# Two halves of the tokens around the inner norms of a two-layer encoder trunk, with half copies on ScalarE and a scaled m in PSUM

## What is computed

```python
h = rms_norm(x, norm_mix_pre[layer])
m = mixer(h, ...)                       # layer 0: RG-LRU and stick-breaking attention; layer 1: windowed GQA
x = x + rms_norm(m, norm_mix_post[layer])
h = rms_norm(x, norm_ffn_pre[layer])
u = causal_dwconv(h @ w_up, conv_w, conv_b)
f = (gelu(u[..., :2816]) * u[..., 2816:]) @ w_down
x = x + rms_norm(f, norm_ffn_post[layer])
```

## Time and profile before

| what | value |
|---|---|
| median of 3 runs | 1190.69 us (1187.4 to 1191.2) |
| the profiled execution | 1188.73 us |
| its span | 1186.9 us |
| granted TensorE clock, mean | 0.993 of full speed |
| TensorE busy | 1149.5 us |
| VectorE busy | 692.9 us |
| ScalarE busy | 486.1 us |
| GpSimd busy | 73.2 us |

### The profile page before, as it was taken

The page is one execution under the profiler, slowest core; times in us unless marked ns, Lnnn a source line. Parts: engine busy times, 40 slices in busy tenths (PEclk is TensorE's granted clock), DMA queues, the critical chain, the costliest instruction groups (busy, mean ns, idle before and its releaser), DMA issues.

```text
span 1186.9 us, 14989 instructions
## 1 busy us (share of the span) xinstructions
PE 1149.5 (97%) x5888; PEld 959.4 (81%) x5888; DVE 692.9 (58%) x840; ACT 486.1 (41%) x667; POOL 73.2 (6%) x57
## 2 busy tenths in 40 slices
PE   8999999999999999999999998899999999999997
PEld 6875777777888888888887788786888888899997
DVE  5745455558876766732228677248877766752222
ACT  4555655434533443431123229334444443433220
POOL 3000000122000000000112100033000000000000
PEclk9999999999999999999999999999999999999999
DMA  6312112222333332322321541041423333332221
GB/s 212 107 36 72 36 36 71 71 72 71 107 84 93 106 104 77 103 98 98 98 98 36 156 129 49 1 126 34 135 79 105 106 88 88 106 98 65 96 99 71
DMA packets 147477, 104.39 MB, mean 88 GB/s; under 512 B 4642, under 2 KB 144354, under 8 KB 147426
## 3 DMA queue, kind: packets, MB, share of 16 engines
q1 hardware_dynamic: 146466, 102.36, 29.0%
q10 hardware_dynamic: 960, 1.31, 0.5%
HBM read 98.02 MB, written 2.10 MB: 84 GB/s over the span
## 4 chain that ended last, share of the span: by engine, by line
PE 84%; DVE 7%; ACT 6%; issue 1%; POOL 0%; DMA 0%; POOLq 0%; SPq 0%; DVEq 0%; ACTq 0%
PE ps L1283 25%; PE ps L1285 25%; PE ps L1284 25%; DVE x L1076 3%; PE ps L1480 2%; PE ps L1468 2%; ACT hx_hi L656 1%; DVE hx_lo L1080 1%; ACT prob L772 1%; PE ps L1491 1%; PE ps L1352 1%; ACT w_hi L522 1%; PE ps L1345 1%; PE ps L1504 1%; PE ps L1660 1%
## 5 line engine op out<-in xcount | busy, mean ns | idle before, releaser
L1283 PE MATMUL ps<-hx_hi,w_hi 128*128 128x512 f32 x912 | 360.5, 395 | 2.7 <-DVE hx_lo L1080 2.5
L1284 PE MATMUL ps<-hx_lo,w_hi 128*128 128x512 f32 x912 | 355.9, 390 | 0.0
L1285 PE MATMUL ps<-hx_hi,w_lo 128*128 128x512 f32 x912 | 355.7, 390 | 0.0
L810 DVE TENSOR_TENSOR w_lo<-w_raw,w_hi 128x2048 fp32r<-128x2048 f32 (+1 forms) x90 | 201.9, 2243 | 169.5 <-ACT w_hi L522 169.4
L522 ACT ACTIVATE w_hi<-w_raw 128x2048 fp32r<-128x2048 f32 (+1 forms) x90 | 168.4, 1871 | 159.2 <-DMA w_raw<-in_ffn_w_down 113.8
L1283 PEld LDWEIGHTS ps<-hx_hi,w_hi 128*128 128x128 f32 x912 | 171.5, 188 | 45.8 <-DVE hx_lo L1080 7.2
L1285 PEld LDWEIGHTS ps<-hx_hi,w_lo 128*128 128x128 f32 x912 | 171.6, 188 | 36.3
L1284 PEld LDWEIGHTS ps<-hx_lo,w_hi 128*128 128x128 f32 x912 | 171.7, 188 | 35.2 <-issue 0.7
L1283 PE MATMUL ps<-w_hi,g_hi 128*128 128x256 f32 x352 | 99.2, 282 | 0.0
L1285 PE MATMUL ps<-w_hi,g_lo 128*128 128x256 f32 x352 | 98.9, 281 | 0.0
L1284 PE MATMUL ps<-w_lo,g_hi 128*128 128x256 f32 x352 | 98.9, 281 | 0.0
(11 more groups left out here) (202 smaller groups left out, 1524.1 us busy)
## 6 DMA issues: line engine op xcount, KB each, us to landing
w_raw<-in_ffn_w_up SPq DMA_DIRECT2D x88, 512.0 KB, 5.0
w_raw<-in_ffn_w_down SPq DMA_DIRECT2D x16, 1024.0 KB, 5.1
w_raw<-in_even_w_in SPq DMA_DIRECT2D x8, 1024.0 KB, 5.1
w_raw<-in_ffn_w_down SPq DMA_DIRECT2D x8, 768.0 KB, 4.4
w_raw<-in_odd_w_qkv SPq DMA_DIRECT2D x6, 1024.0 KB, 5.0
w_raw<-in_even_w_out SPq DMA_DIRECT2D x4, 1024.0 KB, 5.1
w_raw<-in_odd_w_o SPq DMA_DIRECT2D x4, 1024.0 KB, 5.7
x_in<-in_x SPq DMA_DIRECT2D x4, 512.0 KB, 6.4
```

Of the source, the lines that this page charges most:

```text
L810: dve.tensor_tensor(w_lo[s][:, 0:k], w_raw[s][:, 0:k], w_hi[s][:, 0:k], ALU.subtract).then_inc(w_lo_done, 1)
L1283: pe.matmul(dst, s_hi, r_hi, start=first, stop=False)
L1284: pe.matmul(dst, s_hi, r_lo, start=False, stop=False)
L1285: return pe.matmul(dst, s_lo, r_hi, start=False, stop=last)
```

## The change

1. At each boundary the last projection's units (three of four in the mixers; in the down-projection the last three, which make one pair of tiles) run over tokens 0 to 255 first and then over tokens 256 to 511. A half unit writes both column blocks into one bank. The post-norm is done once for each half: its sum and broadcast for the first half stand inside the second half's matmuls (before steps 3 and 5), those for the second half inside the next projection.
2. VectorE's and ScalarE's work on x goes through 8 tiles of 256 tokens for each half. The dummy matmuls are gone.
3. The next projection's first two units run over the first half of the tokens, one after the other, then over the second half, k by k. The pre-norm's sum and broadcast stand inside the third unit (its steps 1 and 6).
4. The half tiles of m are copied by ScalarE, behind the square; the whole tiles still by VectorE.
5. The scaled m is written to the free half of PSUM bank 6 or 7, beside the broadcast that is read from the other half, and added to x from there.
6. The first unit of each up-projection has a slot of its own, in memory left by the attention; its load waits for the attention's last product. Its weights are split during the output projection.
7. The splits at the boundaries stand at other places: the second, third and fourth up unit (first, second and third QKV unit) inside the loops over the 8 tiles. In the FFN, unit 0 splits unit 4, units 1 and 2 split nothing.
8. In layer 0 only the first two output units have an early part; the second one's is in halves. In `sw_values` the head groups alternate between the two row halves.

```diff
+def slot(u):
+
+    if u in U_UP:
+        return RING + U_UP.index(u)
+    return (u - sum(u > x for x in U_UP)) % RING
...
+    sq = [at(f"sq{b}", [P, T], F32, tmp0 + (0, 2, 3)[b] * T * 4) for b in range(3)]
...
     def split_at(layer, u):
 
-        return {0: u + 3, 1: u + 3, 2: None}.get(u - U_UP[layer], u + 2)
+        return {0: u + 4, 1: None, 2: None}.get(u - U_UP[layer], u + 2)
...
+            if layer == 0:
+                sp_.wait_ge(av_mm, SB_HEADS)
+            else:
+                sp_.wait_ge(o_mm, NCH)
+            for j in range(4):
...
+        def half_out(bi, h, j, u):
+
+            i = 3 if bi == 1 else 1 + j
+            half_square(bi, h, j, u)
+            act.activation(m[:, 2 * i:2 * i + 2, tokens_of(h)], halves(bank(group_banks(group_of(u)) + h)),
+                           ACT.Copy).then_inc(group_evac if h else ahalf_evac, 1)
+
+        def boundary(bi, which, layer, last, splits):
+
+            def hi(h, i):
+                act.wait_ge(x_new, 2 * DT * bi + DT * h + i + 1)
+                act.activation(hx_hi[:, i, tokens_of(h)], x[:, i, tokens_of(h)], ACT.Identity,
+                               scale=gain(which, layer, i)).then_inc(hx_hi_done, 1)
+
+            act.preload_act_table_set("sqrt_and_others")
+            for j, v in enumerate(last):
+                half_out(bi, 0, j, v)
+            post_root(bi, 0)
+            if bi != 1:
+                half_out(bi, 1, 0, last[0])
+            for i in range(DT):
+                hi(0, i)
+                if i == (4 if bi == 1 else 3):
+                    split_hi(splits[0])
+                if i == 5 and bi != 1:
+                    half_out(bi, 1, 1, last[1])
+            half_out(bi, 1, len(last) - 1, last[-1])
+            split_hi(splits[1])
+            post_root(bi, 1)
+            for i in range(DT):
+                hi(1, i)
+                square(bi + 1, i, x[:, i, :])
+                if i == (3 if bi == 1 else 5):
+                    split_hi(splits[2])
+            root(bi + 1)
...
+        def boundary(bi, post, pre, last, splits):
+
+            def normed(h, i):
+
+                j = i // 2 - (4 - len(last))
+                if i % 2 == 0 and j >= 0:
+                    if h == 0:
+                        dve.wait_ge(ahalf_evac, a_halves(bi) + j + 1)
+                    else:
+                        dve.wait_ge(group_evac, evacuated(group_of(last[j])))
+                if i:
+                    dve.wait_ge(x_new, 2 * DT * bi + DT * h + i)
+                dve.scalar_tensor_tensor(out=bank(6 + h)[:, HALF:T], in0=m[:, i, tokens_of(h)], scalar=gain(*post, i),
+                                         in1=bank(6 + h)[:, 0:HALF], op0=ALU.mult, op1=ALU.mult).then_inc(post_t, 1)
+
+            def add(h, i):
+
+                dve.wait_ge(post_t, 2 * DT * bi + DT * h + i + 1)
+                dve.tensor_tensor(x[:, i, tokens_of(h)], x[:, i, tokens_of(h)], bank(6 + h)[:, HALF:T], ALU.add).then_inc(x_new, 1)
+
+            def lo(h, i):
+                dve.wait_ge(hx_hi_done, DT + 2 * DT * bi + DT * h + i + 1)
+                dve.scalar_tensor_tensor(out=hx_lo[:, i, tokens_of(h)], in0=x[:, i, tokens_of(h)], scalar=gain(*pre, i),
+                                         in1=hx_hi[:, i, tokens_of(h)], op0=ALU.mult, op1=ALU.subtract).then_inc(hx_ready, 1)
+
+            post_inverse(bi, 0)
+            for h in range(2):
+                dve.wait_ge(pbc_mm, 2 * bi + h + 1)
+                for i in range(2):
+                    normed(h, i)
+                    add(h, i)
+                for i in range(DT):
+                    lo(h, i)
+                    if i + 2 < DT:
+                        normed(h, i + 2)
+                        add(h, i + 2)
+                    if i == 5 and h == 0 and bi == 1:
+                        split_lo(splits[0])
+                    if i == 5 and h == 1:
+                        split_lo(splits[2] if bi == 1 else splits[1])
+                if h == 0:
+                    if bi != 1:
+                        split_lo(splits[0])
+                    post_inverse(bi, 1)
+                    if bi == 1:
+                        split_lo(splits[1])
+            if bi != 1:
+                split_lo(splits[2])
+            inverse_rms(bi + 1)
+            spread(bi + 1)
+            dve.wait_ge(rbc_done, bi + 2)
...
+        def post_mean_square(bi, h):
+
+            if h:
+                pe.wait_ge(pstd_done, 2 * bi + 1)
+            else:
+                pe.wait_ge(std_done, bi + 1)
+            pe.wait_ge(psum_done, post_sums(bi) + (5 if bi == 1 else 5 + 4 * h))
+            q = 6 + h if bi == 1 else 4 + 3 * h
+            pe.wait_ge(psq_done, post_squares(bi) + q + 1)
+            for t in (2 * h, 2 * h + 1):
+                c = P * (t - 2 * h)
+                srcs = (sumsq[:, P * t:P * t + P], sq[q % 3][:, c:c + P], sq[q % 3][:, HALF + c:HALF + c + P])
+                for i, src in enumerate(srcs):
+                    last = pe.matmul(bank(7)[:, t:t + 1], src, ones[:, 0:1], start=i == 0 and t == 2 * h, stop=i == 2 and t == 2 * h + 1)
+            last.then_inc(pms_mm, 1)
+
+        def post_spread(bi, h):
+
+            pe.wait_ge(pdiag_done, 2 * bi + h + 1)
+            if h:
+                pe.wait_ge(pstd_done, 2 * bi + 2)
+            pe.matmul(bank(6 + h)[:, 0:HALF], ones, diag[:, 2 * h:2 * h + 2, :].rearrange("p t c -> p (t c)"),
+                      start=True, stop=True).then_inc(pbc_mm, 1)
...
+        def out_half(layer, j, h, k, first, last):
+
+            u = U_OUT[layer] + j
+            hi, lo = mixer_out(layer, k)
+            for b in range(2):
+                dst = bank(group_banks(group_of(u)) + h)[:, tokens_of(b)]
+                ins = three(dst, *weights(u, k, b), hi[:, tokens_of(h)], lo[:, tokens_of(h)], first and b == 0, last and b == 1)
+            return ins
...
+        def out_halves(layer):
+
+            bi = 2 * layer
+            ks = {1: rest if layer == 0 else range(UK), 2: range(UK), 3: range(UK)}
+            for h in range(2):
+                step = 0
+                for j in (1, 2, 3):
+                    u = U_OUT[layer] + j
+                    if h == 0:
+                        unit_ready(u)
+                        if layer == 1:
+                            banks_free(group_of(u))
+                    for k in ks[j]:
+                        if h and step == 3:
+                            if layer == 0:
+                                pe.wait_ge(group_evac, 1)
+                            post_mean_square(bi, 0)
+                        if h and step == 5:
+                            post_spread(bi, 0)
+                        step += 1
+                        last = out_half(layer, j, h, k, k == 0 and (layer, j) != (0, 1), k == UK - 1)
+                    last.then_inc(unit_done if h else ahalf_mm, 1)
...
+        def first_units(bi, u):
+
+            a_copied, evac = a_halves(bi) + (1 if bi == 1 else 3), evacuated(group_of(u) - 1)
+            pe.wait_ge(ahalf_evac, a_copied)
+            for j in range(2):
+                unit_ready(u + j)
+                for k in range(UK):
+                    if j == 0 and k == 3:
+                        post_mean_square(bi, 1)
+                    if j == 0 and k == 6:
+                        post_spread(bi, 1)
+                    pe.wait_ge(hx_ready, DT + 2 * DT * bi + k + 1)
+                    first_half(u + j, 0, k)
+            pe.wait_ge(group_evac, evac)
+            for k in range(UK):
+                pe.wait_ge(hx_ready, 2 * DT + 2 * DT * bi + k + 1)
+                for j in range(2):
+                    last = first_half(u + j, 1, k)
+                    if k == UK - 1:
+                        last.then_inc(unit_done, 1)
+            unit(u + 2, hx, hooks={(0, 1): lambda: mean_square(bi + 1), (0, 6): lambda: spread(bi + 1)})
...
-            for e in range(8):
+            for e in (0, 4, 1, 5, 2, 6, 3, 7):
```

More of the change, by code:

```diff
@@ L54 @@
 G_SHIFT = N_DOWN - 4
-def n_sums(n):
-    return DT - 1 if n % 2 == 0 else DT - 2
-def sums_before(n):
-    return sum(n_sums(i) for i in range(n))
+HALF = T // 2
+N_BOUNDARY = 3
 V_CONV = 64
@@ L375, in load_cols @@
             slot_free(u)
-            load(u, cols(w, c0), whole(u % RING))
+            load(u, cols(w, c0), whole(slot(u)))
         w_in, w_qkv = io["even_w_in"][0], io["odd_w_qkv"][0]
@@ L477, in _ @@
                     src = w_down[k0 * P:k1 * P, bass.ds(i * 256, 256)].rearrange("(k p) n -> p k n", p=P)
-                    load(u, src, whole(u % RING, k1 - k0))
+                    load(u, src, whole(slot(u), k1 - k0))
         for t in range(TT):
@@ L1532, in _ @@
             sb_av(h)
-        ready = [4, 5, 6]
+        ready, rest = [4, 5, 6], [0, 1, 2, 3, 7]
         unit_ready(U_OUT[0])
@@ L1537, in _ @@
         pe.wait_ge(yb_ready, 6)
-        out_part(0, ready, first=True)
+        out_whole(0, ready, first=True)
         sb_cum(SB_HEADS - 1)
@@ L1552, in _ @@
[L1552 to L1570 removed]
```

(18 more changed lines are left out.)

414 lines of the change are left out of this document (225 added, 189 removed).

## The result

The changed kernel takes 1174.65 us (median; 1173.45 to 1176.66) against 1190.95 for the kernel before on the same chip: ratio 0.987, 95% interval 0.985 to 0.990. That is faster by 16.3 us on the medians and by 14.1 us between the spans of the profiled executions (1172.8 against 1186.9). 1181 was forecast, with a range of 1171 to 1190. The sign and the range held. The reason given for the gain did not, as the experiments show.

A forecast was written before the change was run, and what follows sets the result against it. TensorE bounds the kernel, with 43.0 us lost at three boundaries. Boundaries save 12.9, less 4.0 behind them, plus 1.0 for product order: 9.9 us off 1188.73, forecast 1181 us on the median's scale, range 1171 to 1190.

The forecast's parts named there:

- Half matmuls: Boundaries: 690 more matmuls from splitting into 256 columns, 0.0065 us per split one, 4.5 us lost in all.
- Norm work: Each boundary: half sums, half broadcasts, whole sum and broadcast left on TensorE, 5.7 us, 17.1 us over three.
- (a): Boundary 0: TensorE stalls for ya_lo after the last attention product, the third projection's early part being gone; 1.2 us.
- (b): Last projection's weights, loaded once the first's slot is free, come late: 0.7 us in boundary 0, nothing in boundary 2.
- (c): Between half sum and half broadcast: root, reciprocal and diagonals fit; only 0.3 us where the last square is late.
- (d): Boundary 1: no spare slot, so the first QKV weights are split by 19.0 us, TensorE there at 17.4; 1.7 us.
- (e): Second half of x: hx_lo waits for GpSimd's square sums, so TensorE waits 1.6, 1.4 and 1.6 us at the boundaries.
- QKV wait: Behind boundary 1: the fourth QKV unit's weights come late after the norm's broadcast moves into the third unit; 2.6 us stall.
- Sixth FFN unit: FFN stages: its weights, split in the fourth's turn, are ready 28.3 us on, TensorE there at 27.7; 0.7 us twice.
- Rival 1: VectorE's operations with one PSUM operand also wait for GpSimd: 8 us less gain, 1189 us; chance 0.20 with milder form.
- Rival 2: hx_lo usually precedes GpSimd (+4.7 us) and stalls after the boundary don't come (+4.0): 1172 us; chance 0.17.
- Rivals 3 and 4: 3: VectorE's half tiles cost nearly whole ones, 1205 us, chance 0.07; 4: weights late at (b) and (d), 1185, 0.08.

The follow-up runs named there:

- the FFN move: The changed kernel with the sixth FFN unit's weights split in the third turn in place of the fourth: span 1172.7 us.
- experiment 3: The changed kernel with the scaled half tile written back to m in SBUF, so the add reads two SBUF operands: 1184.79 us, ratio 0.9944.

## Why the prediction was right, and where it was wrong

**What bounds the kernel** held: the time is TensorE's, and only the boundaries moved (rest 135.1 us in all kernels).

**The step that failed** is in "the change, part by part": the scaled m in PSUM was taken as a price only ("a scaled m written to PSUM is shown nowhere, and the same bounds serve"), and the sum let the halves alone win back what it took from the 43.0 us that the boundaries lose. The earlier trace rows already had the hold, the prediction named it, and even cited the rule by which an operation with one SBUF input is not held. But the sum never asked what that part does alone: 0.74 + 0.75 + 0.69 = 2.2 us a tile against TensorE's 2.75. Alone it gives 13.8 us where the whole change gives 14.1. No rival was of this form, that one part alone gives the result and the larger ones add nothing. The sum was laid out for the changed kernel, and most of its terms held there, so the number came near for its own reasons. That the small part alone ends at the same time is a coincidence of two losses, and the forecast could not have told the two apart.

Term by term, in the changed kernel:
- Half matmuls, 0.1176 each forecast: 0.1133 to 0.1200 measured, right in the main.
- Norm work of 5.7 us a boundary: 5.3 to 5.5 measured.
- (a) 1.2: TensorE's interval at ya_lo is 1.16 us, 1.0 of it lost. (b) 0.7: 0.6. (c) 0.3: 0.1 here, 0.5 in the trace of the FFN move.
- (d) 1.7: 1.2.
- (e) 1.6, 1.4, 1.6: 0.8, 0.5, 0.8. This is the largest miss in size, 2.5 us. The last hx_lo of boundary 0 was ready 23.9 us after the projection's start, where 24.8 was forecast, since every other hx_lo met only the end of a sum.
- QKV wait 2.6: an interval of 2.60, 2.4 of it lost, as forecast; the dip of the clock behind it (some 1.5 us) was not in the sum.
- Sixth FFN unit, 0.7 twice: 0.88 and 0.86 from start to start against 0.23, right.
- Order of the products 1.0, with 0 to 2 as bounds: nothing that can be told from 0 (1.8 us faster to 1.1 slower).

The profiled execution gained 14.1 us where the sum had 9.9. The largest parts of the difference are (e), 2.5, and the attention, 2.4 shorter where 1.0 was taken, most of that the execution's.

Rival 1 (held in all three operations) is out by the 48 unvarying adds and 48 unvarying scaled m. Rival 2 (a clear run) came true in part: (e) was halved, what follows the boundary was not. Rivals 3 and 4 did not show: half tiles took 0.48, 0.42 and 0.48 us against the 0.48, 0.44 and 0.48 taken.

## What to carry to other kernels

When a change has several parts, price the smallest one alone first, with the stage's own balance: here one operand moved to PSUM took VectorE's step below TensorE's and left the larger rework nothing to win until three insertion points were mended. Where an elementwise operation reads two SBUF operands beside a GpSimd operation, look at its longest duration against its shortest in the trace. Here a ratio of 2.6 (1.78 to 0.68 us) was a wait that an operand in PSUM, or the GpSimd operation gone, took away.

## What was not expected of the hardware

- Whether the hold falls on an operation is a matter of phase. With a step of 2.14 us GpSimd's sum of 1.34 us fits each time between two hx_lo, and none of 24 is held (0.750 to 0.754 us). With half tiles 20 of the 24 hx_lo of the second halves take 0.70 to 1.55 us where 0.48 is free, though the same three operations take turns.
- The same wait at the fourth QKV unit was followed by 5 us at a granted clock of 0.66 in the first profile and by no fall in the second; of six traces three have the fall. Behind the three pauses of 2.0 to 3.4 us of experiment 3 it fell each time.
- 256-column matmuls have two paces, 0.1133 and 0.1178 us, in the same code from one execution to another, both at a granted clock of 1.00. Over the first halves of layer 1 alone that is 0.7 us. The cause is open.
